# Decay factors of a gated recurrence: a running sum on VectorE in place of matrix products on TensorE

## The reference, cut to what matters

```python
def step(S, xs):
    qc, kc, vc, gc = xs                      # gc: log of the decay per frame and feature
    b = jnp.cumsum(gc, axis=1)
    o_inter = jnp.einsum('bchk,bhkv->bchv', qc * jnp.exp(b), S)
    diff = b[:, :, None] - b[:, None, :]
    decay = jnp.exp(jnp.where(tril[None, :, :, None, None], diff, -jnp.inf))
    scores = jnp.sum(qc[:, :, None] * kc[:, None] * decay, axis=-1)
    o_intra = jnp.einsum('bijh,bjhv->bihv', scores, vc)
    b_last = b[:, -1]
    S = jnp.exp(b_last)[..., None] * S + jnp.einsum(
        'bjhk,bjhv->bhkv', kc * jnp.exp(b_last[:, None] - b), vc)
    return S, o_inter + o_intra
```

## Time and profile before

| | |
|---|---|
| median of 3 runs | 3353.88 us (3353.06 to 3355.38) |
| span of the profiled execution | 3349.8 us, 4.1 us under the median |
| busy, of the span | PE 95%, DVE 44%, ACT 30%, POOL 19% |
| mixer stage of layer 0, 297 to 810 us | PE busy 457 us of 513 |
| mixer stage of layer 1, 1946 to 2460 us | PE busy 455 us of 514 |
| stretch between them (output projection, FFN, next projection) | PE busy 1122 us of 1136 |

### The profile page before, as it was taken

The page is one execution under the profiler, slowest core; times in us unless marked ns, Lnnn a source line. Parts: engine busy times, 40 slices in busy tenths (PEclk is TensorE's granted clock), DMA queues, the critical chain, the costliest instruction groups (busy, mean ns, idle before and its releaser), DMA issues. The chain is left out here.

```text
span 3349.8 us, 50802 instructions
## 1 busy us (share of the span) xinstructions
PE 3183.6 (95%) x19854; PEld 2885.0 (86%) x19854; DVE 1477.6 (44%) x2589; ACT 994.6 (30%) x2077; POOL 638.9 (19%) x951
## 2 busy tenths in 40 slices
PE   6999988988999999999989998898999999999999
PEld 5997666657999999999989966666589999999998
DVE  5312556655443344333372035665545443333443
ACT  4222345444321121211142233553433212111111
POOL 2113656521200000000031145663211000000000
PEclk8999999999999999999999999999999999999999
DMA  6415811103111111111123262111210111111101
GB/s 215 138 68 163 260 41 60 37 17 130 38 51 38 38 42 59 50 38 38 38 79 106 95 197 87 54 52 29 97 64 26 38 63 50 38 38 38 50 25 54
DMA packets 192340, 237.17 MB, mean 71 GB/s; under 512 B 18697, under 2 KB 166494, under 8 KB 192190
## 3 DMA queue, kind: packets, MB, share of 16 engines
q1 hardware_dynamic: 137276, 158.44, 14.7%
q10 hardware_dynamic: 44354, 45.25, 4.3%
q0 software_dynamic: 10560, 31.44, 2.6%
HBM read 195.53 MB, written 39.56 MB: 70 GB/s over the span
## 5 line engine op out<-in xcount | busy, mean ns | idle before, releaser
L1550 PE MATMUL banks<-act_split,w_split 128*128 128x384 f32 (+1 forms) x8352 | 1390.0, 327 | 11.1 <-DVE act_split L2294 11.1
L1550 PEld LDWEIGHTS banks<-act_split,w_split 128*128 128x128 f32 x8352 | 1378.4, 188 | 17.9 <-DVE act_split L2294 10.1
L1550 PE MATMUL banks<-hidden_split,w_split 128*128 128x384 f32 (+1 forms) x3168 | 528.3, 327 | 0.0
L1550 PEld LDWEIGHTS banks<-hidden_split,w_split 128*128 128x128 f32 x3168 | 524.7, 188 | 0.9 <-issue 0.6
L2352 DVE SCALAR_TENSOR_TENSOR x<-banks,mod,x 128x384 f32<-128x384 f32 (+2 forms) x768 | 353.6, 496 | 193.3 <-PE banks L1550 190.8
L2801 DVE TENSOR_TENSOR hidden_f<-banks,silu_a 128x384 f32<-128x384 f32 x132 | 70.7, 535 | 736.4 <-PE banks L1550 736.4
L1550 PE MATMUL banks<-w_split_tm,act_split 128*128 128x396 f32 (+1 forms) x1728 | 317.2, 344 | 0.0
L1550 PEld LDWEIGHTS banks<-w_split_tm,act_split 128*128 128x128 f32 (+1 forms) x1728 | 300.9, 182 | 13.2 <-issue 4.0
L1515 ACT ACTIVATE w_split<-w_raw 128x2048 fp32r<-128x2048 f32 x60 | 112.4, 1906 | 381.3 <-PE banks L1550 381.3
L1509 ACT ACTIVATE hidden_split<-hidden_f 128x384 fp32r<-128x384 f32 x132 | 67.0, 508 | 519.3 <-DVE hidden_f L2801 519.3
L620 POOL TENSOR_TENSOR norm_sum_n<-norm_sum_n,norm_sq 128x384 f32<-128x384 f32 (+1 forms) x42 | 43.3, 1032 | 798.8 <-ACT norm_sq L930 795.0
(11 more groups left out here) (235 smaller groups left out, 3254.7 us busy)
## 6 DMA issues: line engine op xcount, KB each, us to landing
w_raw<-in_w_ffn_in SPq DMA_DIRECT2D x44, 1024.0 KB, 5.1
w_mod_front<-in_w_mod ACTq DMA_DIRECT2D x76, 512.0 KB, 4.9
w_raw<-in_w_ffn_out SPq DMA_DIRECT2D x22, 1024.0 KB, 4.9
z_token_major<-z_stage POOLq DMA_DIRECT2D x64, 198.0 KB, 2.2
r_qkg<-z_feature_major SPq DMA_DIRECT2D x16, 576.0 KB, 4.3
r_v<-z_token_major SPq DMA_DIRECT2D x16, 512.0 KB, 3.7
w_raw<-in_w_o SPq DMA_DIRECT2D x8, 1024.0 KB, 7.1
w_mod_first<-in_w_mod SPq DMA_DIRECT2D x7, 1024.0 KB, 12.0
```

The lines of the kernel that those rows point to most:

```text
L1550: return T.matmul(out, lhsT, rhs, start=start, stop=stop, skip_group_check=True)
```

## The change

The matrix products and the transposes before them are gone. DVE makes one running sum per tile over 3 x 128 columns (`log_sums`, a `tensor_tensor_scan` that starts anew at every 64th column) and a small total. It is put in slot 6 of the tile before, in the place of `g_lo`. For levels 1 to 5 DVE subtracts running sums directly into `r_e` (`spans`: 4 subtractions of 128 x 192 for levels 1 and 2 in slot 7 of the tile before, 6 for levels 3 to 5 in slot 1), and ACT takes the exp in place (`near_decays`: 128 x 192 and 128 x 768 in slot 7, 128 x 1152 in slot 2). For the widest level, the running decay and the decay to the end of the tile, ACT takes the exp of the running sum with a pointer to a bias (`far_decays`: two of 128 x 192 and three of 128 x 64 in slot 4, nine of 128 x 64 in slot 5). The two widest levels of scores are copied onto `r_p` by ACT (`blocks`, two copies in slot 6, one in slot 7), no longer by DVE's predicated copy; PE's `outputs` waits for DVE's fifth mask and ACT's last copy. POOL copies the keys of level 0 where it multiplied them.

```diff
-R_MAT, R_LM = 0, NMAT * P
+R_KEEP, R_LM = 0, 3 * P
...
-                        if h == 0:
-                            sums(g, 0, 1)
-                            sums(g, 0, 2)
-                        else:
+                        if h:
                             levels(g, h - 1)
-                        if h == 1:
-                            sums(g, 1, 0)
-                        elif h == 2:
-                            sums(g, 1, 1)
-                            sums(g, 1, 2)
-                        elif h == 3:
+                        if h == 3:
                             diagonal(g)
-                        elif h == 4:
-                            sums(g, 2, 0)
-                        elif h == 5:
-                            sums(g, 2, 1)
-                            sums(g, 2, 2)
-                        elif h == 6 and g + 1 < NTILE:
-                            log_turn(g + 1)
                         elif h == 7:
                             key_turn(g)
-                            if g + 1 < NTILE:
-                                sums(g + 1, 0, 0)
...
+                def near_decays(g, i):
+                    e = rE[:, (3 * g + i) % 2]
+                    if i == 0:
+                        if g:
+                            wait(act, "r_pool", l, f"q{g - 1}_5")
+                            wait(act, "r_dve", l, f"q{g - 1}_5")
+                        wait(act, "r_dve", l, f"c{g}")
+                        odd = lambda x: x.rearrange("p f (n c) -> p f n c", c=2)[:, :, :, 1]
+                        rstep(S.activation(odd(e[:, 0]), odd(rZ[:, g % 2, 6:9]), ACT.Exp), f"e{g}_01")
+                    wait(act, "r_dve", l, f"d{g}_{i}")
+                    x = e[:, 1 - min(i, 1):3]
+                    rstep(S.activation(x, x, ACT.Exp), f"e{g}_{i}")
...
                         elif h == 7:
+                            blocks(g, 6)
                             wait(act, "r_pe", l, f"kt{g}")
                             rstep(S.activation(rKT[:], ps[R_BANK["kt"]][:, 0:384].rearrange("p (f k) -> p f k", f=3), ACT.Copy),
                                   f"kt{g}")
                             if g + 1 < NTILE:
-                                decay(g + 1, 0, 0)
+                                near_decays(g + 1, 0)
...
+                def log_sums(g):
+                    if g == 0:
+                        dve.wait_ge(rm_ld, (l + 1) * 16)
+                    else:
+                        wait(dve, "r_act", l, f"e{g - 1}_2")
...
+                    rstep(V.tensor_tensor_scan(rC[:].rearrange("p f t -> p (f t)"), rM[:],
+                                               rZ[:, g % 2, 6:9].rearrange("p f t -> p (f t)"), 0.0, ALU.mult, ALU.add),
+                          f"c{g}", True)
+                    rstep(V.tensor_tensor(rTL[:], rC[:, :, 63], rC[:, :, P - 1], ALU.add), f"t{g}")
+
+                def spans(g, i):
+                    e = rE[:, (3 * g + i) % 2]
+                    if i == 0 and g:
+                        wait(dve, "r_pool", l, f"q{g - 1}_5")
+                    elif i == 1 and g:
+                        wait(dve, "r_pool", l, f"k2{g - 1}")
+                    for m in range(1 - i, 3):
+                        b = LEVELS[3 * i + m]
+                        blk = lambda x: x.rearrange("p f (n c) -> p (f n) c", c=2 * b)
+                        c, d = blk(rC[:]), blk(e[:, m])
+                        mid = c[:, :, b - 1:b].broadcast_to([P, 3 * P // (2 * b), b])
+                        rstep(V.tensor_tensor(d[:, :, 0:b], mid, c[:, :, 0:b], ALU.subtract), f"d{g}_{i}l{m}")
+                        rstep(V.tensor_tensor(d[:, :, b:2 * b], c[:, :, b:2 * b], mid, ALU.subtract),
+                              f"d{g}_{i}" if m == 2 else f"d{g}_{i}r{m}")
...
                 def r_mask(i):
                     g, h = divmod(i, 8)
-                    if g < NTILE and h:
+                    if g < NTILE and 1 <= h <= WIDE:
                         masked(g, h - 1)
...
                         if g + 1 < NTILE:
-                            g_lo(g + 1)
+                            log_sums(g + 1)
+                    elif h == 1:
+                        spans(g, 1)
+                    elif h == 7 and g + 1 < NTILE:
+                        spans(g + 1, 0)
```

More of the change, by code:

```diff
@@ L241, in program @@
     rQX = place("r_qx", [P, 8, P], F32, a)
-    rM = place("r_sums", [P, NMAT * P], F32R, a)
-    rGS = place("r_g_split", [P, 2, 3, P], F32R, a)
+    rM = place("r_keep", [P, 3 * P], F32, a)
+    rC = place("r_cum", [P, 3, P], F32, a)
+    rTL = place("r_total", [P, 3], F32, a)
     ZT = place("z_tile", [P, 2, 544], F32, a)
-    assert a[0] == w_end
+    assert a[0] <= w_end
     rQK = place("r_qk", [P, 3, P], F32, [lt_at + 8448, lt_end - 128])
@@ L691, in decayed @@
                     if lv % 3 == 0:
-                        wait(pool, "r_act", l, f"e{g}_{i}2")
+                        wait(pool, "r_act", l, f"e{g}_{i}")
                     if NLEV * g + lv >= 2:
@@ L1049, in load_z, with blocks @@
                     act.dma_start(ZT[0:n, q % 2, :], zt_d[t0:t0 + n, 0:544]).then_inc(a_ld[q % 2], 16)
[L1051 to L1060, removed]
+                def blocks(g, lv):
+                    b = LEVELS[lv]
+                    wait(act, "r_pe", l, f"s{g}_{lv}")
+                    wait(act, "r_dve", l, f"m{g}_{WIDE - 1}")
+                    src = ps[R_BANK[f"s{lv}"]].rearrange("p (h n c) -> p h n c", h=8, c=b)
+                    for n in range(64 // b):
+                        k0 = 2 * b * n
+                        rstep(S.activation(rP[k0:k0 + b, :, k0 + b:k0 + 2 * b], src[k0:k0 + b, :, n], ACT.Copy),
+                              f"m{g}_{lv}" if n == 64 // b - 1 else f"m{g}_{lv}x")
@@ new lines, in near_decays, with far_decays @@
+                    wait(act, "r_dve", l, f"d{g}_{i}")
+                    x = e[:, 1 - min(i, 1):3]
+                    rstep(S.activation(x, x, ACT.Exp), f"e{g}_{i}")
+                def far_decays(g, half):
+                    e = rE[:, (3 * g + 2) % 2]
+                    lo, hi = rC[:, :, 0:64], rC[:, :, 64:P]
+                    if half == 0:
+                        wait(act, "r_pool", l, f"q{g}_2")
+                        wait(act, "r_dve", l, f"q{g}_2")
+                        rstep(S.activation(e[:, 0, :, 64:P], hi, ACT.Exp), f"e{g}_2r")
+                        rstep(S.activation(e[:, 1, :, 0:64], lo, ACT.Exp), f"e{g}_2b")
+                        for f in range(3):
+                            rstep(S.activation(e[:, 0, f, 0:64], lo[:, f], ACT.Exp, scale=-1.0, bias=rC[:, f, 63:64]), f"e{g}_2k{f}")
+                    else:
+                        wait(act, "r_dve", l, f"t{g}")
+                        for f in range(3):
+                            rstep(S.activation(e[:, 1, f, 64:P], hi[:, f], ACT.Exp, bias=rC[:, f, 63:64]), f"e{g}_2q{f}")
+                        for f in range(3):
+                            rstep(S.activation(e[:, 2, f, 0:64], lo[:, f], ACT.Exp, scale=-1.0, bias=rTL[:, f:f + 1]), f"e{g}_2l{f}")
+                        for f in range(3):
+                            rstep(S.activation(e[:, 2, f, 64:P], hi[:, f], ACT.Exp, scale=-1.0, bias=rC[:, f, P - 1:P]),
+                                  f"e{g}_2" if f == 2 else f"e{g}_2m{f}")
@@ L1268, in _ @@
                 load_mod(S, l, 1)
[L1269 removed]
+                near_decays(0, 0)
                 for i in range(24):
@@ L1673, in claim @@
                         wait(pe, reader[b][0], l, reader[b][1])
[L1675 to L1682, removed]
                 s = st("zt_pe")
@@ L1715, in _ @@
                                        f"gate{c}")
[L1716 to L1721, removed]
-                    if i == 0 and f == 0:
-                        wait(pe, "r_dve", l, f"gl{g}")
-                    claim(b)
-                    for a_ in range(2):
-                        ins = mm(ps[b][:, 0:384], rGS[:, a_, f], rM[:, 384 * i:384 * i + 384], a_ == 0, a_ == 1)
-                    rs.done(ins, f"d{g}_{i}{f}")
-                    reader[b] = ("r_act", f"e{g}_{i}{f}")
                 def levels(g, lv):
@@ L2493, in decayed @@
                     if lv % 3 == 0:
-                        wait(dve, "r_act", l, f"e{g}_{i}2")
+                        wait(dve, "r_act", l, f"e{g}_{i}")
                     if lv == 0:
@@ L2622, in _ @@
                 t8, n8 = ORDER[0], DEC_SEQ
-                g_lo(0)
+                log_sums(0)
+                wait(dve, "zt_pe", l, "t3_7")
+                spans(0, 0)
                 step(V.memset(GQC[NOPE:QK], 1.0), "gone")
```

69 lines of the change are left out of this document (23 added, 46 removed).

## The result

The changed kernel takes 3406.72 us (median of 4 runs, 3401.75 to 3410.43) against 3354.63 us for the kernel before: a ratio of 1.0156, 95% interval 1.0144 to 1.0168. The profiled execution has a span of 3405.1 us, 55 us more than before, at a mean granted clock of 0.965, where the kernel before had 0.984.

The account below looks back on a forecast made before the run. It took PE's work to bound the front tiles and a loop of waits between engines the attention tiles. Layer terms of +1.85 and +1.25 gave +3.1 us, a span of 3352.9, plus 4.1 for the median: 3357 us, range 3315 to 3382.

Parts of the forecast that it names:

- the wait at the end of q = 0: Last transpose beside tile q = 0, behind subtractions and exp in the second turned queries' way: some 2.7 us later.
- the waits for `q_t` at the narrow turns: Turn to the next narrow tile: first scores wait for the second turned queries, 1.6 to 2.0 us late.
- `k_tm` at 3 us or more: Sign in the profile: beside tile 2, PE's wait for POOL's `k_tm`, 1.90 us before, grows to 3 or more.
- the first front tile of layer 0: First front tile, where PE is full: removed PE work less a slot 1 delay, -2.8 us in either layer.
- the front, "+0.3 net": Front slots 1 and 2: 1.7 us of subtractions ahead of `mod_copy`, against 1.4 us of PE work removed.
- +1.65 in the sum: Attention tile q = 0: delays by scan, subtractions and exp, less PE work removed, +1.65 us in each layer.
- the 0.45 of the forecast: Slot 6 beside q = 0: the scan in `g_lo`'s place lengthens PE's 1.68 us pause by 0.45 us.
- the clock, +0.9 a layer: Longer PE pauses at key turns and tile turns: one more lower-clock stretch a layer, +0.9 us (0 to 3).
- The lower clock spreads: Rival: three lower-clock stretches a layer instead of one, +3.5 us, within the first case's range; no chance of its own.
- The narrow tiles, +4.2 in the sum: Attention tiles q = 1 to 4: +1.05 us each from slot 1 subtractions and the late turn, +4.2 per layer.
- PE sets the pace: Rival: removed PE work pays in the attention tiles too, -45 us, 3309 us; chance 0.35.
- The subtractions meet POOL: Rival: DVE's subtractions cost 0.81 us each beside POOL, +52 us, or 3383 us if half meet it; chance 0.29.

Follow-up runs that it names:

- e8: The kernel before without the second of the two matmuls of each sum of log decays, nothing added: 3350.5 us, ratio 0.9997.
- e11: The changed kernel, order untouched, with matmuls that nobody reads put into pauses that the change made or lengthened: 3391.36 us, ratio 1.0117.
- e6: e4 plus matmuls that nobody reads, ahead of the second scores beside tile 0 and the key turn beside tiles 1 to 3: 3339.79 us.
- e4: The changed kernel with the subtractions and running sum moved later in their slots, and two exps into the next tile's slot 0: 3349.75 us.
- e5: e4 with ACT's two exps of the next tile at the tile's end, behind the turned queries and narrow output copy: 3340.27 us.

## Why the prediction was wrong

I forecast 3357 us, no change, with 3315 to 3382 as the range; the kernel takes 3407. Against the sum, the front tiles of both layers together are out by 19 us, the two tiles q = 0 by 16 and the narrow tiles by 12, 47 in all.

- **What held.** The price of a subtraction (0.34 us, one every 0.27), of the exp (0.84 for 0.90), the wait at the end of q = 0 (2.87 us where it was 0.24, so 2.6 later; I forecast some 2.7, and its own terms give 2.6), the waits for `q_t` at the narrow turns (2.08, 1.86, 1.64 and 1.43 us beside q = 1 to 4 of layer 0; forecast 1.6 to 2.0), `k_tm` at 3 us or more, and the first front tile of layer 0 (-2.9 us, forecast -2.8; in layer 1 only -0.3). That the removed PE work pays nothing beside the narrow tiles is what e8 shows, there and for the whole kernel.
- **The step that failed first: the front, "+0.3 net".** I set 1.7 us of delay against 1.4 us of PE work removed. Both lengthen the same pause, and 0.20 us of wait became 2.53: the turn of the rows started 5.81 us after the first mask, where it had been 4.19, so the delay of 1.6 us was paid in full, and the work removed only brought PE 0.7 us earlier to the wait. The clock behind the pause cost more than the delay: 0.33 on the turn itself (0.94 for 0.61), 0.86 + 0.86 on the next two groups and 1.23 on the four matmuls after them, 3.3 us, against a wait for weights of 0.86 that was gone. In all the level of slot 3 came 3.9 us later in this tile; in the third tile it was 4.5 us, and 4.4 and 1.0 in layer 1.
- **The step that was missing: slot 1 beside q = 0 and q = 5.** I knew that `r_slot` stands ahead of the second copy there, and used it for the scan in slot 6 and not for the six subtractions in slot 1. The next level came 2.9 us later in q = 0 of both layers and 2.8 in q = 5 of layer 0. Tile q = 0 was +1.65 in the sum and is +7.9 and +11.5. In slot 6, where I did count the scan, it was mis-sized: the pause grew by 1.63 us (1.68 to 3.31) and not by the 0.45 of the forecast, with the scan at 1.77 us for 0.9.
- **The term that was mis-sized: the clock, +0.9 a layer.** I counted one stretch. I had named it as a rival too, "The lower clock spreads", and priced it at 3.5 us. Beside q = 0 the granted clock fell from 0.96 to 0.88 and 0.80, beside q = 2 from 1.00 to 0.92. e11 puts some 15 us on it in both layers together, where I had 1.8, and e6 shows 10 us from two kinds of pause alone. The narrow tiles, +4.2 in the sum and +10.1 and +10.4 measured, had the waits that I forecast and this clock on top.
- **The rivals.** "PE sets the pace" is out: e8. "The subtractions meet POOL" came near the time, at its full price (3409), for a wrong reason: the mean price was 0.41 us and not 0.81. By the Trainium skill's page "SBUF — State Buffer", section "Who interferes with whom", a subtraction of two SBUF inputs and a POOL instruction that reads SBUF go by turns. The trace agrees: of the 180 subtractions, 160 took 0.34 to 0.36 us, all but one of them with POOL at rest or setting a buffer to a constant, and the 20 that met a product or a copy of POOL took 0.61 to 1.88. But little hung on it, since they were so few. The scan is where it bites: 1.77 us at 463.96.

The Trainium skill's page "TensorE: Matmul & The Clock Gate", section "HAM oscillation — how this bites in real kernels", warns that matmuls which keep pausing start each burst at the lower clock. The traces here agree, with pauses that other engines make and not DMAs: 1.93 us for 1.07 at 351.22. It spoke for a larger clock term than the one stretch a layer that I took.

## What to carry to other kernels

Before moving work from a busy engine to idle ones, look at what stands behind the new instruction in its queue and which engine waits for that; a gap in the busy share isn't a free place. When the waiting engine comes earlier too, don't subtract that from the delay: the delay is paid in full, and the pause, behind which the clock falls, grows by both. And where TensorE pauses behind other engines, price its clock with each pause: the same change lost 52 us in one order, gained 13 in another, and 25 with matmuls that nobody reads in the pauses that were left.

## What the hardware showed that I had not expected

- More work made the kernel faster: ten filler matmuls (two instructions each) in each layer's pauses took 10 us off e4, 11 off e5 and 7 off the kernel before.
- An addition of 128 x 3 took 0.48 us on average (0.16 to 0.82, median 0.39), right behind the scan whose end it reads; a subtraction of 128 x 192 took 0.35 with POOL at rest.
- A scan of 128 x 384 took 1.22 us on average: 0.94 to 0.95 beside the narrow tiles, and 1.48 to 1.77 where it met POOL's products. `g_lo` of the same width took 0.545.
